# Sixteen modulation columns in a feed-forward: single-column sums on TensorE against transposes and a sum on VectorE

## The chip, the cores and the metric

The kernel runs on one core of one Trainium2 chip. The metric is the device time of one execution in microseconds (us). A core has five engines that run their own instruction streams and wait for each other through semaphores: PE (TensorE, matrix products into the eight PSUM banks), DVE (VectorE), ACT (ScalarE), POOL (GpSimd) and SP (SyncE, which here only issues transfers).

## The reference, cut to what matters

Two two-layer blocks with a width of 1024 follow each other on 512 tokens. Each layer multiplies and shifts its input by vectors that come from a condition vector `c` through a large matrix. The feed-forward of each layer of the first block is followed by a norm whose output is modulated by the *next* layer's first two vectors:

```python
c_act = jax.nn.silu(c)
for i in range(DEPTH):
    mods = jnp.split(c_act @ w_ada[i] + b_ada[i], 6, axis=-1)
    sh1, sc1, g1, sh2, sc2, g2 = [m[:, None, :] for m in mods]
    u = x * (1.0 + sc1) + sh1
    ...
    x = layer_norm(DEEPNORM_ALPHA * x + (1.0 + g1) * y, ln_g[i, 0], ln_b[i, 0])
    u = x * (1.0 + sc2) + sh2
    y = squared_relu_mlp(u, ff_w1[i], ff_w2[i])
    x = layer_norm(DEEPNORM_ALPHA * x + (1.0 + g2) * y, ln_g[i, 1], ln_b[i, 1])
```

The second block (`ada_w_2`, `ada_b_2`) uses shift, scale and gate in the same way after an RMS norm.

## The kernel before, in words

**Products.** Every float32 product is made of three TensorE passes (`PASSES`), with weights and activations split into a high and a low part. Weights come in halves of 512 rows by 512 columns: SP loads `raw`, ACT makes the high part (`act_high`, L191), POOL the low part (L2462), PE uses both (`wsp`), and `w_used` frees the slot.

**Modulation.** The product of `c` and the modulation matrix is not made on TensorE alone. While a feed-forward runs, DVE accumulates row block after row block, times the elements of silu(c), into `modacc[l]` (128 partitions by 6144 columns, L711). What is left is the sum over the 128 partitions. For shift and scale it must come out as *columns* (element on the partition), 16 blocks of 128 for each feed-forward. `pe_modcols` (L718) makes each with one product of the block with a column of ones; the trace has two records (passes) for each of these float32 products. For gates it must come out as *rows* on all partitions: `pe_modrow` (L724), ones times the accumulator.

**End of a feed-forward.** `pe_ff(l)` ends with `down_pair`: the last two blocks of the hidden layer (operands `hT` and `xT`) are multiplied into the two column halves n = 0 and n = 1 of the output, four token tiles t each. For n = 0 the results lie in banks 4 to 7, for n = 1 in banks 0 to 3; a tile of n = 1 is 24 products (L493). `down_tile` weaves the 16 `pe_modcols` into the 24 products of tile 0 of n = 1, one ahead of each of the first 16. They write bank 4, so PE waits for `ada_used` (all of `modacc` is there) and for `acc_done` of tile 0 of n = 0 (DVE is done with bank 4). The last one raises `mod_done`.

**DVE beside it.** `dve_ff` handles the tiles in the order that PE makes them: `add_pair(n, t)` adds what was accumulated (L652), multiplies by the gate (L653), adds the residual (L654), raises `acc_done` and takes norm statistics (L767). Between the four tiles of n = 0 and the four of n = 1 stands `before_pair`: `next_columns` waits for `mod_done` and adds the bias to the 16 columns from bank 4 (L2616), then a few operations on 8 columns fold them with the norm's scale and bias (L775 to L778 in the first feed-forward, L2630 to L2632 in the second), and `mod_made` is raised. The last tile of n = 1 has its sum prepared (`settled`) and begins with L653. In the second feed-forward alone, each tile of n = 1 is followed by `affine1` on DVE (L2674 and L2676, 1024 columns each), with which ACT makes the RMS norm.

**After it.** PE waits for `mod_made`, then does `pe_modrow` for both gates, and in the second feed-forward, once DVE has done `acc_done` of the very last tile, 16 further `pe_modcols` (L550). Then `pe_transposes_by_tile` turns the normed tokens (L339), in the second feed-forward with a wait for `mod_made` before k = 3, which DVE raises after another `next_columns` and the four operations of `next_rows` (L2625). After the transposes the products of the next stage start (L233).

Of the kernel before, what the change touches and what calls it, by code (L numbers as in the profile page):

```python
# [12 lines left out]
P = 128  # L13
# [34 lines left out]
def build(nc, T, out):  # L48
# [8 lines left out]
    with ctx:  # L57
# [43 lines left out]
        def col(name, k=0, n=1):  # L101
            return cols[:, ROWS[name] + k:ROWS[name] + k + n]
# [305 lines left out]
        def sp_ff(sp, l, ada, rows):  # L408
# [44 lines left out]
            for n in range(2):  # L453
                for q in range(2):
                    k = (FB - 2 + q) * HK
                    sp_half(sp, b + 4 * FB - 4 + 2 * n + q, q, W2[l][:, k:k + HK, n * COLS:n * COLS + COLS])
                    if n == 0:
                        ada_tiles(FB - 1, range(4 + 2 * q, 6 + 2 * q))

        def pe_ff(pe, l):  # L460
            s = FS[f"ff{l}"]
            b = base[f"ff{l}"]
            ts = TS[f"hid_ff{l}"]

            def up(m, peel=False):

                j = b if peel else b + 4 * m - 2
                if peel:
                    first_half(pe, j, "T", ts["bank_free"], 0, ts)
                for h in range(1 if peel else 0, 2):  # L470
                    for t in range(4):
                        if h == 0:
                            pe.wait_ge(s["sq_done"], 4 * m - 4 + t + 1)
                        for k in range(HK):
                            if t == 0:
                                low_ready(pe, j + h, k)
                            if peel and t == 0:
                                pe.wait_ge(ts["xT_ready"], ts["k0"] + HK * h + k + 1)
                            mm = pe_tile(pe, bank[t][:, :], h, k, HK * h + k, t, "T", h == 0 and k == 0,
                                         h == 1 and k == HK - 1)  # L480
                        if h == 1 and t < 3:
                            mm.then_inc(s["ff1_tile"], 1)
                    mm.then_inc(w_used, 1)

            def down_tile(h, j, slot, t, bk, start=True, stop=True, columns=()):
                for k in range(HK):
                    if t == 0:
                        low_ready(pe, j, k)
                    for q, (a, c) in enumerate(PASSES):
                        n = 3 * k + q  # L490
                        if n < len(columns):
                            pe_modcols(pe, modacc[l], columns[n:n + 1], ST, mod_done if columns[n] == 15 else None)
                        mm = pe.matmul(bank[bk][:, :], h[:, a, k, t * P:t * P + P], wsp[:, slot, c, k, :],  # L493
                                       start=(start and k == 0 and q == 0), stop=(stop and k == HK - 1 and q == 2))
                return mm

            def down(i, peel=False):

                j = b + 4 * i + 4
                pe.wait_ge(s["hT_ready"], 4 * i + 4)  # L500
                for n in range(2):
                    for t in range(ST):
                        if not (peel and n == 0):
                            pe.wait_ge(s["acc_done"], 8 * i + 4 * n - 4 + t + 1)
                        mm = down_tile(hT[l], j + n, n, t, ST + t)
                        mm.then_inc(s["ff2_tile"] if t < 3 else w_used, 1)

            def down_pair():

                i, j = FB - 2, b + 4 * FB - 4  # L510
                for q, h in enumerate((hT[l], xT)):
                    pe.wait_ge(s["hT_ready"], 4 * (i + q) + 4)
                    for t in range(ST):
                        if q == 0:
                            pe.wait_ge(s["acc_done"], 8 * i - 4 + t + 1)
                        mm = down_tile(h, j + q, q, t, ST + t, q == 0, q == 1)
                        if t == ST - 1:
                            mm.then_inc(w_used, 1)
                        elif q == 1:
                            mm.then_inc(s["ff2_tile"], 1)  # L520
                pe.wait_ge(s["sq_done"], 4 * FB)
                for t in range(ST):
                    for q, h in enumerate((hT[l], xT)):
                        columns = ()
                        if t == 0:
                            if q == 0:
                                pe.wait_ge(s["ada_used"], KT * FB)
                                pe.wait_ge(s["acc_done"], 8 * i + 1)
                            columns = (range(12), range(12, 16))[q]
                        mm = down_tile(h, j + 2 + q, q, t, t, q == 0, q == 1, columns)  # L530
                        if t == ST - 1:
                            mm.then_inc(w_used, 1)
                        elif q == 1:
                            mm.then_inc(s["ff2_tile"], 1)

            up(0, peel=True)
            up(1)
            down(0, peel=True)
            with pe.Fori(1, FB - 2) as i:
                up(i + 1)  # L540
                down(i)
            up(FB - 1)
            down_pair()
            pe.wait_ge(mod_made, (5, 8)[l])
            for r, off in enumerate(mod_rows[l]):
                pe.wait_ge(s["acc_done"], 8 * (FB - 2) + 2 * r + 2)
                pe_modrow(pe, modacc[l], off, ST + 2 * r, mod_done)
            pe.wait_ge(s["acc_done"], 8 * (FB - 2) + 2 * ST)
            if l:
                pe_modcols(pe, modacc[l], range(24, 40), HK - 1, mod_done, at=SEQ - P)  # L550
# [2008 lines left out]
        def _(dve):  # L2559
# [52 lines left out]
            def next_columns(at, bk, bias, done, off=0):  # L2612

                c = slice(at, at + 16)
                dve.wait_ge(mod_done, done)
                dchain(dve, dve.tensor_tensor(modcol[:, c], bank[bk][:, off + at:off + at + 16], bias, ALU.add))  # L2616

            def next_rows(l, one, done):

                dve.wait_ge(brow_ld, 32 * l + 32)  # L2620
                for r, gate in enumerate((gate1, gate2)):
                    dve.wait_ge(mod_done, done + r)
                    for n in range(2):
                        c = slice(n * COLS, n * COLS + COLS)
                        dchain(dve, dve.scalar_tensor_tensor(gate[:, c], bank[4 + 2 * r + n][:, :], one, brow[l][:, r, c], ALU.add, ALU.add))  # L2625
                dve.sem_inc(mod_made, 1)
# [14 lines left out]
            ready = TS["in_att_in"]["tok_ready"]  # L2641

            def before_pair0():
                next_columns(0, ST, col("b_ada", 48, 16), 5)
                dve_fold(dve, 0, 1, 0, 8)
                dve.sem_inc(mod_made, 1)
            dve_ff(dve, 0, 0, 1, gate2, 32, before_pair0, None)
# [16 lines left out]
            dve_transposed(dve, "hid_ff1")  # L2664

            def before_pair1():
                next_columns(0, ST, col("ada_b_2", 0, 16), 9)
                rms_fold(0)
                dve.sem_inc(mod_made, 1)
                dve.wait_ge(ln_ld, 128)  # L2670
# [75 lines left out]
```

## Time and profile before

| | us |
|---|---|
| median of 3 runs | 1802.36 |
| lowest and highest of them | 1799.96 and 1802.83 |
| the profiled execution's own time | 1807.33 |
| its span, first to last instruction | 1805.6 |
| mean granted TensorE clock of the span | 0.991 of full |

In the timeline each row is a group of like instructions: its start, the time to the end of the group, engine, line and operation, the tile written and those read, and how many. In square brackets stands how long the engine had been idle, and what ended that. PE is the product itself, PEld the loading of its stationary operand, which overlaps with the product before. Products are pipelined, so consecutive products start closer together than one takes. An engine's name with a q is its instruction queue.

### The profile page before, as it was taken

Reading aid. Unit: us, or ns where it says so; the run is one execution under the profiler, and the core shown is the slowest. Engines: PE = TensorE matmul, PEld = TensorE weight load, DVE = VectorE, ACT = ScalarE, POOL = GpSimd, SP = SyncE. Lnnn points to the kernel's source line nnn. Section 1 sums busy time; section 2 is a strip of 40 time slices with the busy share of each in tenths; the row PEclk is TensorE's granted clock in tenths of the full one; section 3 lists DMA queues with packets and bytes.
Section 4 is the critical chain, followed back from the end, with each engine's and each line's share of the span. In section 5 each row is a group of like instructions: output and inputs, shape, how many; then the busy total and the mean of one; then the engine's idle time right before and its main releaser. Section 6 shows DMA issues by size and latency. Waiting matters only on the chain.

```text
span 1805.6 us, 24893 instructions
## 1 busy us (share of the span) xinstructions
PE 1759.9 (97%) x9203; PEld 1445.3 (80%) x9203; DVE 1092.5 (61%) x1644; ACT 759.4 (42%) x1193; POOL 766.9 (42%) x577
## 2 busy tenths in 40 slices
PE   6999999999999999999999999999999999999999
PEld 5776677888888887888788888888888887887887
DVE  6876556656665772754475566568388845347742
ACT  3443336222222253664432222235444456665551
POOL 4523234555555354222355555552432334441222
PEclk9999999999999999999999999999999999999999
DMA  9643424655555323222275555542221132232211
GB/s 329 237 151 107 162 94 140 221 163 165 174 167 196 124 94 114 85 82 67 74 261 177 172 175 167 175 153 71 94 70 54 47 95 93 94 94 82 71 59 70
DMA packets 132219, 235.79 MB, mean 131 GB/s; under 512 B 8560, under 2 KB 48368, under 8 KB 132128
## 3 DMA queue, kind: packets, MB, share of 16 engines
q1 hardware_dynamic: 129088, 227.21, 38.3%
q10 hardware_dynamic: 3040, 7.34, 1.2%
q8 instruction: 61, 1.00, 0.2%
q14 instruction: 30, 0.25, 0.0%
HBM read 232.39 MB, written 2.13 MB: 130 GB/s over the span
## 4 chain that ended last, share of the span: by engine, by line
issue 44%; POOL 29%; PE 23%; DVE 3%; ACT 1%; POOLq 0%; DVEq 0%; ACTq 0%
POOL wsp L2462 29%; PE bank L233 12%; PE bank L1462 2%; PE bank L1428 2%; PE bank L1430 1%; PE bank L2009 1%; PE bank L1550 1%; PE bank L1538 1%; PE bank L1504 1%; PE bank L1763 0%; DVE hst L2248 0%; ACT fP L1584 0%; PE bank L1780 0%; DVE hE L2205 0%; DVE hX L2216 0%
## 5 line engine op out<-in xcount | busy, mean ns | idle before, releaser
L2462 POOL TENSOR_TENSOR wsp<-raw,wsp 128x512 fp32r<-128x512 f32 x528 | 758.9, 1468 | 1018.9 <-ACT wsp L191 1018.9
L233 PE MATMUL bank<-xT,wsp 128*128 128x512 f32 x2592 | 603.2, 392 | 4.3 <-ACT xT L379 2.7
L233 PEld LDWEIGHTS bank<-xT,wsp 128*128 128x128 f32 x2592 | 488.2, 189 | 109.7 <-DVE xT L385 3.2
L191 ACT ACTIVATE wsp<-raw 128x2048 fp32r<-128x2048 f32 x132 | 252.7, 1915 | 484.2 <-PE bank L493 240.8
L493 PE MATMUL bank<-wsp,hT 128*128 128x512 f32 x1344 | 313.4, 391 | 0.0
L233 PE MATMUL bank<-wsp,xT 128*128 128x512 f32 x1248 | 300.9, 396 | 2.2 <-POOL wsp L2462 2.0
L493 PEld LDWEIGHTS bank<-wsp,hT 128*128 128x128 f32 x1344 | 252.4, 188 | 51.4
L233 PEld LDWEIGHTS bank<-wsp,xT 128*128 128x128 f32 x1248 | 231.5, 189 | 55.7 <-issue 4.5
L634 DVE TENSOR_TENSOR x<-bank,x 128x512 f32<-128x512 f32 x80 | 55.3, 691 | 117.1 <-PE bank L493 116.7
L618 DVE TENSOR_TENSOR hT<-h,hT 128x512 fp32r<-128x512 f32 x56 | 90.5, 1674 | 23.4 <-ACT hT L568 23.4
L1428 PE MATMUL bank<-xT,wsp 128*128 128x512 f32 x384 | 99.3, 403 | 2.0 <-DVE gT L1930 2.0
L711 DVE SCALAR_TENSOR_TENSOR modacc<-ada_ring,csil,modacc 128x768 f32<-128x768 f32 (+1 forms) x80 | 91.5, 1143 | 3.4
L385 DVE TENSOR_TENSOR xT<-u,xT 128x512 fp32r<-128x512 f32 x64 | 65.0, 1036 | 44.5 <-ACT xT L379 44.3
L563 ACT ACTIVATE h<-bank 128x512 f32<-128x512 f32 x64 | 38.4, 599 | 114.3 <-PE bank L233 114.3
L1428 PEld LDWEIGHTS bank<-xT,wsp 128*128 128x128 f32 x384 | 68.9, 188 | 19.0 <-issue 2.9
L607 DVE TENSOR_TENSOR h<-bank,h 128x512 f32<-128x512 f32 x64 | 42.8, 686 | 65.6 <-ACT h L563 65.6
L711 DVE SCALAR_TENSOR_TENSOR tok<-ring,csil,tok 128x512 f32<-128x512 f32 x56 | 53.8, 960 | 10.5 <-DMA ring<-in_w_ada 5.0
L1430 PE MATMUL bank<-wsp,xT 128*128 128x256 f32 x384 | 50.0, 286 | 0.0
L1430 PEld LDWEIGHTS bank<-wsp,xT 128*128 128x128 f32 x384 | 46.9, 191 | 1.4 <-issue 1.4
L493 PE MATMUL bank<-wsp,xT 128*128 128x512 f32 x192 | 46.8, 393 | 0.0
L1584 ACT ACTIVATE fP<-fP,f_max 128x256 f32<-128x256 f32 (+3 forms) x64 | 35.3, 553 | 23.8 <-DVE f_max L1634 23.8
L1634 DVE CUSTOM_DVE_ANT_0 aP<-bank,abt 128x256 f32<-128x256 f32 (+3 forms) x64 | 27.5, 487 | 26.9 <-PE bank L1504 26.6
(319 smaller groups left out, 2044.1 us busy)
## 6 DMA issues: line engine op xcount, KB each, us to landing
raw<-in_ff_w SPq DMA_DIRECT2D x64, 1024.0 KB, 5.4
ada_ring<-in_w_ada SPq DMA_DIRECT2D x48, 384.0 KB, 3.8
ada_ring<-in_ada_w SPq DMA_DIRECT2D x48, 384.0 KB, 3.8
ring<-in_w_ada SPq DMA_DIRECT2D x64, 256.0 KB, 3.2
raw<-in_odd_w_in SPq DMA_DIRECT2D x16, 1024.0 KB, 5.5
raw<-in_gla_w_in SPq DMA_DIRECT2D x12, 1024.0 KB, 6.9
raw<-in_att_w_in SPq DMA_DIRECT2D x12, 1024.0 KB, 5.1
raw<-in_even_w_in SPq DMA_DIRECT2D x12, 1024.0 KB, 5.1
```

The source lines that it names most:

```text
L191: act.activation(wsp[:, slot, 0], raw[:, slot], ACT.Copy).then_inc(hi_made, 1)
L233: mm = pe.matmul(out_ap, l, r, start=(start and n == 0), stop=(stop and n == 2))
L385: dve.tensor_tensor(xT[:, 1, k], u32[:, k % 2], xT[:, 0, k].bitcast(F32), ALU.subtract)\
L493: mm = pe.matmul(bank[bk][:, :], h[:, a, k, t * P:t * P + P], wsp[:, slot, c, k, :], start=(start and k == 0 and q == 0), stop=(stop and k ...
L563: act.activation(h32[l][:, t], bank[t][:, :], ACT.Relu).then_inc(s["relu_done"], 1)
L607: dve.tensor_tensor(h32[l][:, t], bank[t][:, :], h32[l][:, t], ALU.mult).then_inc(s["sq_done"], 1)
L618: dve.tensor_tensor(h[:, 1, t], h32[l][:, t], h[:, 0, t].bitcast(F32), ALU.subtract)\
L634: ins = dve.tensor_tensor(y, bank[4 + t][:, :], y, ALU.add)
L711: ins = dve.scalar_tensor_tensor(acc, w, c, acc, ALU.mult, ALU.add)
L1428: mm = pe.matmul(bank[D_BANK][:, :], w[:, i * P:i * P + P], xT[:, a, k, :], start=start, stop=stop)
L1430: mm = pe.matmul(bank[D_BANK][:, 0:COLS // 2], xT[:, a, k, i * P:i * P + P], w, start=start, stop=stop)
L2462: ins = pool.tensor_tensor(wsp[:, slot, 1, k], raw[:, slot, k], wsp[:, slot, 0, k].bitcast(F32), ALU.subtract)
```

## The change

In both feed-forwards of the first block the 16 single-column products are no longer woven into tile 0 of n = 1. Instead PE transposes the 16 blocks of `modacc`, four to a bank, into banks 4 to 7, between tile 0 and tile 1 of n = 1. Each bank waits for the `acc_done` of its own tile of n = 0. DVE sums each transposed block along its free axis, with one `tensor_reduce` for a bank, and then adds the bias. The other 32 uses of `pe_modcols` (16 in the attention stage, 16 at the end of the second feed-forward) stay.

```diff
+        def pe_blocks_turned(pe, acc, bk, n):
+
+            for b in range(4 * n, 4 * n + 4):
+                at = b % 4 * P
+                mm = pe.transpose(bank[bk][:, at:at + P], acc[:, b * P:b * P + P], ident[:, :])
+            return mm
+
...
-            def down_tile(h, j, slot, t, bk, start=True, stop=True, columns=()):
+            def down_tile(h, j, slot, t, bk, start=True, stop=True):
                 for k in range(HK):
                     if t == 0:
                         low_ready(pe, j, k)
                     for q, (a, c) in enumerate(PASSES):
-                        n = 3 * k + q
-                        if n < len(columns):
-                            pe_modcols(pe, modacc[l], columns[n:n + 1], ST, mod_done if columns[n] == 15 else None)
...
                 pe.wait_ge(s["sq_done"], 4 * FB)
                 for t in range(ST):
+                    if t == 1:
+                        pe.wait_ge(s["ada_used"], KT * FB)
+                        for n in range(ST):
+                            pe.wait_ge(s["acc_done"], 8 * i + n + 1)
+                            mm = pe_blocks_turned(pe, modacc[l], ST + n, n)
+                        mm.then_inc(mod_done, 1)
                     for q, h in enumerate((hT[l], xT)):
-                        columns = ()
-                        if t == 0:
-                            if q == 0:
-                                pe.wait_ge(s["ada_used"], KT * FB)
-                                pe.wait_ge(s["acc_done"], 8 * i + 1)
-                            columns = (range(12), range(12, 16))[q]
-                        mm = down_tile(h, j + 2 + q, q, t, t, q == 0, q == 1, columns)
+                        mm = down_tile(h, j + 2 + q, q, t, t, q == 0, q == 1)
...
+            def first_columns(bias, done):
+
+                dve.wait_ge(mod_done, done)
+                for n in range(ST):
+                    blocks = bank[ST + n].rearrange("p (b n) -> p b n", n=P)
+                    ins = dve.tensor_reduce(modcol[:, 4 * n:4 * n + 4], blocks, AX, ALU.add)
+                dchain(dve, ins)
+                dchain(dve, dve.tensor_tensor(modcol[:, 0:16], modcol[:, 0:16], bias, ALU.add))
+
...
             def before_pair0():
-                next_columns(0, ST, col("b_ada", 48, 16), 5)
+                first_columns(col("b_ada", 48, 16), 5)
...
             def before_pair1():
-                next_columns(0, ST, col("ada_b_2", 0, 16), 9)
+                first_columns(col("ada_b_2", 0, 16), 9)
```

## Rows read from the trace of the kernel before

**Rows 1.** The page, busy time and share of the span by engine.

```profile
PE 1759.9 (97%) x9203; PEld 1445.3 (80%) x9203; DVE 1092.5 (61%) x1644; ACT 759.4 (42%) x1193; POOL 766.9 (42%) x577
```

**Rows 2.** Timeline of the first feed-forward's end, PE and DVE.

```profile
611.53 0.28 PE L718 MATMUL bank<-ones,modacc 128*128 128x1 f32 x2
...
617.34 0.69 DVE L654 SCALAR_TENSOR_TENSOR tok<-tok,bank 128x512 f32<-128x512 f32 x1
...
618.33 0.28 PE L718 MATMUL bank<-ones,modacc 128*128 128x1 f32 x2
...
618.79 0.17 DVE L2616 TENSOR_TENSOR modcol<-bank,cols 128x16 f32<-128x16 f32 x1
...
620.63 2.89 PE L493 MATMUL bank<-wsp,hT 128*128 128x512 f32 x12
620.84 0.70 DVE L652 TENSOR_TENSOR bank<-bank,x 128x512 f32<-128x512 f32 x1 [1.06 <-PE bank L493]
...
626.08 2.88 PE L493 MATMUL bank<-wsp,hT 128*128 128x512 f32 x12
626.28 0.70 DVE L652 TENSOR_TENSOR bank<-bank,x 128x512 f32<-128x512 f32 x1 [2.13 <-PE bank L493]
...
637.16 0.70 DVE L653 TENSOR_TENSOR bank<-bank,gate 128x512 f32<-128x512 f32 x1 [2.13 <-PE bank L493]
...
640.39 1.91 PE L339 MATMUL bank<-ident,tok 128*128 128x128 f32 x16
```

**Rows 3.** Timeline of the second feed-forward's end, PE and DVE.

```profile
1222.29 0.28 PE L718 MATMUL bank<-ones,modacc 128*128 128x1 f32 x2
...
1229.55 0.17 DVE L2616 TENSOR_TENSOR modcol<-bank,cols 128x16 f32<-128x16 f32 x1
...
1231.66 0.70 DVE L652 TENSOR_TENSOR bank<-bank,x 128x512 f32<-128x512 f32 x1 [1.33 <-PE bank L493]
...
1237.41 0.69 DVE L652 TENSOR_TENSOR bank<-bank,x 128x512 f32<-128x512 f32 x1
...
1247.72 3.59 PE L724 MATMUL bank<-modacc,ones 128*128 128x512 f32 x8
...
1248.88 0.69 DVE L653 TENSOR_TENSOR bank<-bank,gate 128x512 f32<-128x512 f32 x1
...
1249.61 0.69 DVE L654 SCALAR_TENSOR_TENSOR tok<-tok,bank 128x512 f32<-128x512 f32 x1
...
1251.15 3.63 PE L718 MATMUL bank<-ones,modacc 128*128 128x1 f32 x32
...
1252.68 1.28 DVE L2676 SCALAR_TENSOR_TENSOR x<-tok,rstd,lnrow 128x1024 f32<-128x1024 f32 x1
...
1254.82 0.17 DVE L2616 TENSOR_TENSOR modcol<-bank,cols 128x16 f32<-128x16 f32 x1 [0.85 <-PE bank L718]
...
1255.03 2.87 DVE L2625 SCALAR_TENSOR_TENSOR gate<-bank,brow 128x512 f32<-128x512 f32 x4
...
1258.00 4.53 PE L339 MATMUL bank<-ident,tok 128*128 128x128 f32 x20 [0.68 <-DVEq L2626]
...
1262.19 28.09 PE L233 MATMUL bank<-xT,wsp 128*128 128x512 f32 x122
```

**Rows 4.** Groups by line and form, and one timeline row: prices on DVE.

```profile
L767 DVE BATCH_NORM_STATS2 stats<-tok 128x6 f32<-128x512 f32 x32 | 22.2, 695 | 1.1
...
L2274 DVE TENSOR_TENSOR_SCAN u<-ones,hu 128x512 f32<-128x512 f32 x4 | 4.9, 1215 | 0.0
...
1273.84 0.48 DVE L2181 MEMSET u<- 128x512 f32 x1 [0.17 <-DVE omlb L2175]
```

**Rows 5.** Windows: stretch, length, busy time by engine, granted clock, DMA.

```profile
640.00:645.00 5.00, 4.66 (x37) 4.06 (x36) 3.47 (x6) 4.93 (x9) 3.96 (x4) 1.00 0.00 0
...
1255.50:1256.00 0.50, 0.36 (x3) 0.08 (x1) 0.47 (x2) 0.47 (x2) 0.50 (x1) 0.65 0.00 0
...
1262.00:1262.50 0.50, 0.50 (x4) 0.50 (x3) 0.00 (x0) 0.50 (x2) 0.00 (x0) 0.52 1.05 410
```

## The prediction

> **What bounds the kernel now.** I read the page first: PE is busy for 97% of the span [rows 1], so the first question about any edit is what it does to PE's stream. Then I read the timeline at the end of each feed-forward, because the edit acts at two places only, and asked there which wait ends last.
>
> In the first feed-forward PE goes from product to product without a gap, and DVE waits for it: 1.06 us before tile 0 of n = 1, 2.13 us before tile 1 and 2.13 us before the last one [rows 2]. PE sets the pace. A tile of n = 1 takes PE 626.08 - 620.63 = 5.45 us; DVE needs 3.3 us for it (626.28 - 2.13 - 620.84).
>
> In the second feed-forward it is the other way round. DVE has `affine1` behind each tile, so that its tiles start 1237.41 - 1231.66 = 5.75 us apart, more than PE's 5.45, and DVE idles only ahead of the first, 1.33 us [rows 3]. From there to the end of the feed-forward DVE has no rest. After it the path is: DVE's last tile, PE's 16 late column sums (1251.15, which could not start before `acc_done` of L654, ended 1250.30), DVE's L2616 (it waited 0.85 us for them), L2625 until 1257.90, and only then PE's 20 transposes and the next stage at 1262.19 [rows 3]. So a microsecond saved on PE counts in the first feed-forward, while in the second one added on DVE before 1231.66 counts.
>
> **What is removed.** 16 column sums, 32 passes, from each feed-forward. Tile 0 of n = 1 takes 620.63 - 611.53 = 9.10 us instead of 5.45 [rows 2], so they cost 3.65 us, 0.114 us a pass. The 32 passes that stand alone took 3.63 us [rows 3], the same price, so the weaving hides nothing and costs nothing. DVE's bias add remains.
>
> **What is added on PE.** 16 transposes of 128 x 128. The nearest row is the 16 float32 transposes of `tok`, 1.91 us from first start to last end [rows 2]. A single one took about 0.28 us, but they overlap: (1.91 - 0.28) / 15 = 0.11 us from one to the next, so 16 displace 1.8 us. I take 1.8 us and as bounds 1.7 and 2.2 (if a switch between products and transposes costs some tenths). Saved on PE: 3.65 - 1.8 = 1.85 us in each feed-forward.
>
> A rule speaks against this: the Trainium skill, page "TensorE: Matmul & The Clock Gate", Part 4 (PE-mode transpose), gives about 275 ns for a transpose in a kernel. Taken as the displaced time that would be an estimated 4.4 us for 16, dearer than the 3.65 us removed, and the first feed-forward would lose 0.75 us. The trace has that length for one record but not from start to start, so I keep the row.
>
> **The new waits on PE.** The fourth bank waits for `acc_done` of tile 3 of n = 0, whose L654 ended at 618.03 [rows 2]. Without the woven passes tile 0 ends at 611.53 + 5.45 = 616.98; twelve transposes later, at 618.3, the thirteenth is due. The bank is free 0.3 us earlier: no stall. The second feed-forward has the same distances, with tile 0 starting at 1222.29 [rows 3]. If DVE were later than that, tiles 1 to 3 of n = 1 would queue behind the wait, and DVE's tile 1 behind them.
>
> **What is added on DVE.** Four reductions over 512 float32 from PSUM. The trace before has no such operation. Near rows: operations with 512 columns took 0.69 to 0.70 us, from PSUM too (L652) [rows 2, 4]. Below stands a write of 512 without reading, 0.48; above stands a scan with its serial dependence, 1.215 [rows 4]. I take 0.69, because a sum along the axis reads a column per step as the statistics (0.695) do: 2.8 us for four, bounds 1.9 and 4.9. The wait moves as well: the last transpose ends at 616.98 + 1.8 + 0.2 = 619.0. Then 2.8, bias add and fold (619.78 - 618.79 = 1.0 for L2616 to L778, which end 1.06 us ahead of 620.84) give 622.85, where DVE can take tile 0 of n = 1. It began it at 620.84, so it is 2.0 us late.
>
> **First feed-forward: -1.85 us.** PE's tile 1 is ready for DVE at 626.28 - 1.85 = 624.43, DVE comes at 626.15 (622.85 + 3.3); tile 2 is ready at about 629.9 and DVE is free at 629.5: it has caught up. The last tile begins 1.85 us earlier. Even with reductions of 1.215 us (2.1 us more) DVE would be free at 634.9, ahead of the last tile at 637.16 - 1.85 = 635.3. The cover is thick here. Everything behind it up to the second feed-forward is triggered by PE and its followers (the weight transfers too, through `lo_made`), so it shifts as a whole.
>
> **Second feed-forward, with the clock as it was: +1.3 us.** Times are on the old axis. The last transpose ends at 1222.29 + 5.45 + 1.8 + 0.2 = 1229.75, the reductions at 1232.55, bias and three fold operations 0.8 later, and tile 0 starts at 1233.4 against 1231.66: +1.75 us. With 5.75 us a tile and no rest, the last tile is late by the same: L654 ends at 1252.05 instead of 1250.30, L2676 at 1255.7 instead of 1253.96. PE, 1.85 us early, ends its row sums (L724) at 1249.45 and then *waits* for that `acc_done`: a gap of 2.6 us that was not there. The 32 passes then run from about 1252.5 to 1256.1, L2616 follows at 1256.1 instead of 1254.82, and with it L2625 and PE's 20 transposes: +1.3 us. Of DVE's 1.75 us the old idle 0.85 hid the rest. PE's 1.85 us is lost in the new gap.
>
> **The clock in that gap: +2.0 us.** The granted clock fell to 0.5 (1.2 GHz) at about 1255.8 and came back at 1262.2 to 1262.5 [rows 5]. Before it fell PE had finished its wide products at 1251.3 and done only single columns and transposes. In it the 20 transposes took 4.53 us, twice the 0.11 us each. Now the wide products end 1.85 us earlier. If the clock falls as long after them as it did (4.5 us), that is at 1253.95, when about 2.1 us of the late column sums are still to do; at half clock those take twice as long, +2.1. If it falls as late as before it costs nothing; if it falls before the sums, 3.6. I take 2.0.
>
> **Sum.** -1.85 + 1.3 + 2.0 = +1.5 us. Against the profiled execution's own time that is 1807.3 to 1808.8; this execution lies 5.0 us above the median of the runs, so on the median it is 1802.4 + 1.5 = 1803.9. From no change a measurement of this kernel tells about 0.2%, 3.6 us.
>
> **Rivals.**
> 1. *Both feed-forwards gain.* DVE's delay in the second is hidden after all and PE's 1.85 us counts twice: -3.7 us, 1798.7. For it: DVE idles 1.33 us before tile 0 of n = 1 [rows 3]. Against it: the delay of 1.75 is reckoned after that idle time, and no rest follows. Chance 0.05.
> 2. *The clock stays out of it*, or is back earlier for the 20 transposes (2.3 instead of 4.5 us): -0.55 to -2.7 us, 1799.7 to 1801.8. For it: the moment of the fall can differ from one execution to the next. Chance 0.15.
> 3. *The reductions are slow, and this ends slower.* DVE's price decides: each 0.1 us above 0.69 adds 0.4 us in the second feed-forward. From 1.2 us on a reduction the total passes +3.6 us; at the scan's 1.215 it is 1.5 + 2.1 = +3.6 us, 1806.0, and still above if the first tile is late as well. Against it: three kinds of operation with 512 columns took 0.69. Chance 0.08.
> 4. *The clock falls ahead of the late sums and stays low through the transposes:* 3.6 instead of 2.0, and up to 1.5 us more until it is back: +3.1 to +4.6 us, 1805.5 to 1807.0. Chance 0.12.
> 5. *The transposes themselves make the clock fall within tile 1 of n = 1.* If one tile of n = 1 fell to 1.2 GHz for its 5.45 us, half of that would be lost work, 2.7 us: the first feed-forward's gain is gone, +4.2 us in all, 1806.6. The transposes between 640 and 645, in which PE did little else, ran at a granted 1.00 [rows 5], and here only half as many stand between wide products. Chance 0.03.
>
> The page named above says in the same part that transposes do not count as TensorE being busy for the clock gate. By that rule the fifth rival would be likelier; the trace shows a stretch of transposes at full clock, and a fall where waits stood beside them.
>
> **How the numbers follow.** The forecast, the sums caught in part by the fall, has 0.57 and holds -0.55 to +3.1 us. With rivals 2 and 4 and the halves of 3 and 5 that stay below 3.6 us the middle is thick: within 0.2% 0.83. Faster by over 0.2% is rival 1 and a little of 2: 0.05. Slower is the upper part of 3, 4 and 5: 0.12. The range goes from 1799.8 (rival 2's lower part) to 1806.6 (rival 4's upper part); it leaves out rival 1 and the slow tail, and what other executions' clock elsewhere adds.
>
> **What the changed profile would show.** L718 with 64 records instead of 128; two bursts of 16 transposes at about 1.8 us; tile 0 of n = 1 at 5.45 us; four reductions at 0.69 us each; in the first feed-forward no idle PE and DVE waiting again from tile 2; in the second DVE's four tiles with no idle time, PE idle for 2.6 us ahead of the late L718, and these at more than 0.114 us a pass if the clock fell in them. Wrong are: the sign, if DVE's L652 of the second feed-forward starts at less than 1.3 us late; the size, if a reduction is not near 0.69 us or the fall is elsewhere; the first step, if PE stalls on the fourth bank.

## The result, and the profile after

The changed kernel is slower: 1811.72 us median of 6 runs (1809.1 to 1814.0) against 1802.46 us for the kernel before (6 runs, 1799.72 to 1804.05). The ratio is 1.0047, 95% interval 1.0035 to 1.006. The forecast was 1803.9 us, the range 1799.8 to 1806.6 us, and the likeliest outcome no change beyond 0.2%. The time is above all of it, and there is a change. The first line of the page shows nothing of this; PE is even busy for 2 us less than before [rows 1]:

```profile
PE 1757.9 (97%) x9171; PEld 1443.3 (80%) x9171; DVE 1096.2 (61%) x1652; ACT 759.7 (42%) x1193; POOL 768.0 (42%) x577
```

The profiled execution's span is 1808.7 us, 3.1 us above that of before. Both spans hold what the clock did to unchanged code, so I compare *stages*: a stage here is the stretch from DVE's first gate product of n = 0 (L653, in the changed kernel L657) to the first product of what follows (L233), once for each feed-forward. For before, four further rows of the timeline give both starts, the end of the first stage and, between them, POOL:

```profile
607.85 0.70 DVE L653 TENSOR_TENSOR bank<-bank,gate 128x512 f32<-128x512 f32 x1
...
613.78 4.99 POOL L2462 TENSOR_TENSOR wsp<-raw,wsp 128x512 fp32r<-128x512 f32 x4 [4.30 <-ACT wsp L191]
...
644.36 1.86 PE L233 MATMUL bank<-xT,wsp 128*128 128x512 f32 x7
...
1218.61 0.70 DVE L653 TENSOR_TENSOR bank<-bank,gate 128x512 f32<-128x512 f32 x1
```

The two stages take 644.36 - 607.85 = 36.51 us and, with the last row of [rows 3], 1262.19 - 1218.61 = 43.58 us. Now the timeline of the changed kernel at the end of the first feed-forward:

```profile
602.12 0.70 DVE L657 TENSOR_TENSOR bank<-bank,gate 128x512 f32<-128x512 f32 x1
...
605.80 2.88 PE L497 MATMUL bank<-wsp,hT 128*128 128x512 f32 x12
...
608.06 5.00 POOL L2466 TENSOR_TENSOR wsp<-raw,wsp 128x512 fp32r<-128x512 f32 x4 [4.29 <-ACT wsp L191]
...
609.39 0.96 PE L497 MATMUL bank<-wsp,xT 128*128 128x512 f32 x3 [0.70 <-POOL wsp L2466]
...
610.63 0.96 PE L497 MATMUL bank<-wsp,xT 128*128 128x512 f32 x3 [0.28 <-POOL wsp L2466]
...
611.87 0.96 PE L497 MATMUL bank<-wsp,xT 128*128 128x512 f32 x3 [0.28 <-POOL wsp L2466]
...
613.11 0.97 PE L497 MATMUL bank<-wsp,xT 128*128 128x512 f32 x3 [0.27 <-POOL wsp L2466]
...
613.92 1.91 PE L464 MATMUL bank<-ident,modacc 128*128 128x128 f32 x16
615.58 3.01 PE L497 MATMUL bank<-wsp,hT 128*128 128x512 f32 x12
615.93 2.48 DVE L2627 TENSOR_REDUCE modcol<-bank 128x4 f32<-128x512 f32 x4 [2.91 <-PE bank L464]
...
632.23 0.70 DVE L657 TENSOR_TENSOR bank<-bank,gate 128x512 f32<-128x512 f32 x1 [2.13 <-PE bank L497]
...
639.44 0.94 PE L233 MATMUL bank<-xT,wsp 128*128 128x512 f32 x3
```

Read the four rows of PE with "POOL wsp" at their end. The second half of tile 0 needs the low parts of a weight half that POOL makes one by one, in pieces k = 0 to 3 of three products each, and PE now waits ahead of each piece. Tile 0 takes 613.92 - 605.80 = 8.12 us, not 5.45. POOL works at the same times as before, counted from DVE's first gate product: it begins 5.94 us after it (before 613.78 - 607.85 = 5.93) and ends 10.94 us after it (before 10.92). Tile 1 begins at 13.46 us instead of 620.63 - 607.85 = 12.78. The stage takes 639.44 - 602.12 = 37.32 us: 0.81 us more, where 1.85 less was forecast.

The second feed-forward:

```profile
1215.44 0.70 DVE L657 TENSOR_TENSOR bank<-bank,gate 128x512 f32<-128x512 f32 x1
...
1226.41 0.97 PE L497 MATMUL bank<-wsp,xT 128*128 128x512 f32 x3 [0.28 <-POOL wsp L2466]
...
1227.22 1.91 PE L464 MATMUL bank<-ident,modacc 128*128 128x128 f32 x16
...
1229.23 2.48 DVE L2627 TENSOR_REDUCE modcol<-bank 128x4 f32<-128x512 f32 x4 [2.90 <-PE bank L464]
...
1232.77 0.70 DVE L656 TENSOR_TENSOR bank<-bank,x 128x512 f32<-128x512 f32 x1 [0.23 <-DVE bcol L2645]
...
1249.98 0.69 DVE L657 TENSOR_TENSOR bank<-bank,gate 128x512 f32<-128x512 f32 x1
...
1251.45 5.87 PE L722 MATMUL bank<-ones,modacc 128*128 128x1 f32 x32 [2.53 <-DVE tok L658]
...
1257.36 0.17 DVE L2620 TENSOR_TENSOR modcol<-bank,cols 128x16 f32<-128x16 f32 x1 [2.29 <-PE bank L722]
...
1260.55 3.56 PE L339 MATMUL bank<-ident,tok 128*128 128x128 f32 x20 [0.56 <-DVEq L2639]
...
1263.86 2.32 PE L233 MATMUL bank<-xT,wsp 128*128 128x512 f32 x9
```

DVE takes its first tile of n = 1 at 1232.77 - 1215.44 = 17.33 us instead of 13.05, 4.28 us late, and has no idle time from there to the end of its last tile. That tile is late by the same, PE waits 2.53 us for it, and the late column sums start 36.01 us after the first gate product instead of 32.54 and take 5.87 us instead of 3.63. The 20 transposes behind them are faster by 0.9 us. The stage takes 48.42 us, 4.84 more. The windows show the granted clock in it (the last number but two of a line, 1.00 for 2.4 GHz and 0.50 for 1.2 GHz):

```profile
1252.00:1252.50 0.50, 0.50 (x7) 0.50 (x6) 0.43 (x4) 0.50 (x1) 0.00 (x0) 1.00 0.00 0
1252.50:1253.00 0.50, 0.50 (x6) 0.50 (x5) 0.50 (x2) 0.49 (x2) 0.00 (x0) 0.71 0.00 0
...
1262.50:1263.00 0.50, 0.50 (x5) 0.50 (x4) 0.50 (x1) 0.50 (x2) 0.00 (x0) 0.55 0.95 365
...
1389.00:1389.50 0.50, 0.50 (x6) 0.50 (x5) 0.50 (x2) 0.00 (x0) 0.00 (x0) 0.74 0.13 33
```

The clock falls to 1.2 GHz at about 1252.7, early in the late sums, and is back at about 1262.9. The last line is a further fall, near 1389, in code that the change does not touch. The first fall has not moved toward the start of the stage: it lies 37.3 us after the first gate product, in before at 37.0. It is the late sums that have moved into it.

### The profile page after: what moved, and what is told of

It is laid out like the page before. It is cut to its first block, busy times and chain, and to the rows that moved or that the text cites. A ratio compares the mean times of both kernels' runs of the same rounds, so it can differ in the third digit from the quotient of the medians.

```text
span 1808.7 us, 24837 instructions
## 1 busy us (share of the span) xinstructions
PE 1757.9 (97%) x9171; PEld 1443.3 (80%) x9171; DVE 1096.2 (61%) x1652; ACT 759.7 (42%) x1193; POOL 768.0 (42%) x577
## 3 DMA queue, kind: packets, MB, share of 16 engines
HBM read 232.39 MB, written 2.13 MB: 130 GB/s over the span
## 4 chain that ended last, share of the span: by engine, by line
issue 43%; POOL 29%; PE 22%; DVE 3%; ACT 1%; POOLq 0%; DVEq 0%; ACTq 0%
POOL wsp L2466 29%; PE bank L233 11%; PE bank L1466 2%; PE bank L1432 2%; PE bank L1434 1%; PE bank L2013 1%; PE bank L1554 1%; PE bank L1542 1%; PE bank L1508 1%; PE bank L1767 0%; DVE hst L2252 0%; ACT fP L1588 0%; PE bank L1784 0%; DVE hE L2209 0%; DVE hX L2220 0%
## 5 line engine op out<-in xcount | busy, mean ns | idle before, releaser
L233 PE MATMUL bank<-xT,wsp 128*128 128x512 f32 x2592 | 602.8, 392 | 4.3 <-ACT xT L379 2.8
L233 PEld LDWEIGHTS bank<-xT,wsp 128*128 128x128 f32 x2592 | 488.1, 189 | 108.9 <-DVE xT L385 2.9
L497 PE MATMUL bank<-wsp,hT 128*128 128x512 f32 x1344 | 308.5, 389 | 0.0
L233 PE MATMUL bank<-wsp,xT 128*128 128x512 f32 x1248 | 300.0, 395 | 2.3 <-POOL wsp L2466 2.0
L233 PEld LDWEIGHTS bank<-wsp,xT 128*128 128x128 f32 x1248 | 230.7, 188 | 55.5 <-issue 4.5
L1434 PEld LDWEIGHTS bank<-wsp,xT 128*128 128x128 f32 x384 | 46.9, 191 | 1.4 <-issue 1.4
L497 PEld LDWEIGHTS bank<-wsp,xT 128*128 128x128 f32 x192 | 35.4, 188 | 13.4 <-POOL wsp L2466 6.5
L1588 ACT ACTIVATE fP<-fP,f_max 128x256 f32<-128x256 f32 (+3 forms) x64 | 35.2, 553 | 23.8 <-DVE f_max L1638 23.8
```

The lines of the kernel that those rows point to most:

```text
L233: mm = pe.matmul(out_ap, l, r, start=(start and n == 0), stop=(stop and n == 2))
L1434: mm = pe.matmul(bank[D_BANK][:, 0:COLS // 2], xT[:, a, k, i * P:i * P + P], w, start=start, stop=stop)
```

## The experiments

Stages in us from the timelines, as above; "first tile" is DVE's start of n = 1 in the second feed-forward after its first gate product; "between" and "behind" are the stretches between the stages and from the second one to the end. Ratios with 95% intervals; behind them stand runs of before on the same chip, with medians of 1802.5 to 1803.7 us.

| kernel | stage 1 | between | first tile | stage 2 | behind | ratio to before |
|---|---|---|---|---|---|---|
| before | 36.51 | 574.25 | 13.05 | 43.58 | 543.41 | |
| after | 37.32 | 576.00 | 17.33 | 48.42 | 544.84 | 1.0047 (1.0035 to 1.006) |
| same_again | 36.51 | 573.84 | 13.05 | 43.48 | 543.26 | 1.0007 (0.9995 to 1.0019) |
| one_column | 35.52 | 575.83 | 12.06 | 42.59 | 543.89 | 1.0011 (0.9996 to 1.0026) |
| only_first | 37.31 | 573.86 | 13.05 | 43.53 | 543.25 | 1.0014 (1.0004 to 1.0023) |
| only_second | 36.51 | 573.76 | 17.33 | 48.41 | 544.92 | 1.0032 (1.0018 to 1.0045) |
| in_tile | 35.55 | 575.48 | 14.80 | 44.26 | 544.73 | 0.9999 (0.9988 to 1.0009) |
| in_tile_first | 35.57 | 574.43 | 13.05 | 43.57 | 543.37 | 1.0001 (0.999 to 1.0011) |
| no_reduce | 37.29 | 573.71 | 14.81 | 44.26 | 544.78 | 1.0015 (1.0004 to 1.0027) |
| after_again | 37.32 | 575.65 | 17.32 | 48.40 | 544.81 | 1.0048 (1.0035 to 1.0061) |
| filled_gap | 37.28 | 575.96 | 17.32 | 48.41 | 544.83 | 1.0033 (1.0014 to 1.0052) |
| extra_reduce | 36.51 | 571.96 | 14.47 | 43.91 | 544.82 | 1.0014 (1.0001 to 1.0027) |
| one_reduce | 36.51 | 573.83 | 13.05 | 43.54 | 544.69 | 1.0009 (0.9994 to 1.0024) |
| eight_reduce | 36.51 | 571.97 | 16.98 | 48.04 | 543.13 | 1.0035 (1.002 to 1.0051) |

The stages come out alike within 0.1 us wherever their code is alike, which no whole time does. The conclusions rest on them.

**same_again**, the kernel before without an edit.

> The kernel before, unchanged, as a control. Expected: a ratio of 1.000 within 0.1%. Question: do the stretches at 1.2 GHz in its trace fall at the same places as in the first trace of before (150 to 164, 229 to 236, 283 to 287, 836 to 839, 894 to 898, 1256 to 1262)? If they are tied to the place in the program, the same six are seen. If they are a matter of the single execution, some are missing, and the span differs from 1805.6 us by what they cost.

The stages are the same, the falls of the clock are not: those near 157 and 283 us are missing, one near 101 is new, and its span is 1801.7 us against 1805.6. The falls in the unchanged first 600 us are a matter of the execution. The four traces of before, below, have spans of 1799.1 to 1805.6 us, so that a single span tells nothing of a difference below some 6 us.

**one_column**: is the removed work worth anything?

```diff
-                            columns = (range(12), range(12, 16))[q]
+                            columns = ((), range(15, 16))[q]
```

> The kernel before with 15 of the 16 woven column sums left out in both feed-forwards (only column 15 is made, ahead of the first product of tile 0's second half; the other columns keep whatever the bank held). Theory POOL: the weave stands in a hole in which PE would wait for POOL's low halves anyway, so leaving out 30 passes (3.4 us) shortens tile 0 of n = 1 by only about 1 us (9.1 to about 8.1 us), PE is seen waiting for POOL in its second half, and the kernel is about 2 us faster in all. Rival, the prediction's step: tile 0 shrinks by 3.4 us to about 5.7 us, DVE starts the tiles of n = 1 earlier by up to 1.3 us, and the kernel is 5 us faster.

PE in the first feed-forward:

```profile
605.95 2.88 PE L493 MATMUL bank<-wsp,hT 128*128 128x512 f32 x12
...
609.53 0.38 PE L718 MATMUL bank<-ones,modacc 128*128 128x1 f32 x2 [0.70 <-POOL wsp L2462]
...
613.25 0.96 PE L493 MATMUL bank<-wsp,xT 128*128 128x512 f32 x3 [0.27 <-POOL wsp L2462]
614.05 2.89 PE L493 MATMUL bank<-wsp,hT 128*128 128x512 f32 x12
```

Tile 0 takes 614.05 - 605.95 = 8.1 us with 3.4 us less to do. Both stages are 0.99 us shorter, no more. So the removed weave was worth 1.0 us of PE's time in each feed-forward, not 3.65. The 2 us that this should save in all do not appear in the timing, and noise does not cover them: they would be a ratio of 0.9989, below the interval. The trace has 575.83 us between the stages, where a fall of the clock near 830 lasts 6.8 us instead of the 3.4 us in before; whether that goes with this kernel or with the one execution is open.

**only_first** and **only_second**: the change in one feed-forward alone, by `l == 0` or `l == 1` around the new lines, the woven sums in the other.

> The change in the first feed-forward alone. Theory POOL: tile 0 of n = 1 takes 8.3 us because its second half waits for POOL, the transposes come behind that, and the start of the attention stage's products is 0.75 us later, measured from the start of tile 0; the kernel is 0.5 to 2.5 us slower, the rest by where the clock falls. Rival, the prediction's step: 1.85 us faster.

> The change in the second feed-forward alone. Theory: nearly all of the loss is here. DVE starts the tiles of n = 1 about 4.5 us late (2.9 us wait of PE for POOL, 1.8 us for transposes and 2.5 us for reductions, less 2.7 us that the weave used beyond), stays late by the same because it has no rest, and with the late column sums partly at 1.2 GHz the next stage starts 5 us later: kernel 5 to 7 us slower. Rival: the loss lies in stretches at 1.2 GHz elsewhere, then this kernel is under 3 us slower.

The stages are those of the changed kernel in the edited feed-forward and those of before in the other. The first costs 0.8 us, the second 4.8 to 4.9, and the ratios stand in the same order.

**in_tile**: the transposes inside tile 0.

```diff
             for k in range(HK):
+                if turn:
+                    turn(k)
                 if t == 0:
                     low_ready(pe, j, k)
...
+                def turn(n):
+                    pe.wait_ge(s["acc_done"], 8 * i + n + 1)
+                    mm = pe_blocks_turned(pe, modacc[l], ST + n, n)
+                    if n == ST - 1:
+                        mm.then_inc(mod_done, 1)
...
-                        mm = down_tile(h, j + 2 + q, q, t, t, q == 0, q == 1)
+                        mm = down_tile(h, j + 2 + q, q, t, t, q == 0, q == 1, turn if t == 0 and q == 1 else None)
```

> The changed kernel with the transposes moved into tile 0 of n = 1: the four of bank n stand ahead of the products with k = n of the second half, where PE waits for POOL's low halves. Theory POOL: they are hidden in those waits. Tile 0 takes 8.1 us, as with one woven column; the first feed-forward's stage (from DVE's first L653 of n = 0 to the next stage's first product) takes 35.5 us instead of 37.3 with the change and 36.5 before. In the second, DVE starts the tiles of n = 1 2.9 us earlier than with the change and the stage takes 44.5 to 45.5 instead of 48.4 (before 43.5). Kernel within 0.1% of before. Rival (transposes cost their 1.8 us wherever they stand): 37.3 stays in the first.

```profile
610.55 2.89 PE L499 MATMUL bank<-wsp,hT 128*128 128x512 f32 x12
...
614.94 0.60 PE L464 MATMUL bank<-ident,modacc 128*128 128x128 f32 x4
...
615.38 0.96 PE L499 MATMUL bank<-wsp,xT 128*128 128x512 f32 x3
...
618.67 2.91 PE L499 MATMUL bank<-wsp,hT 128*128 128x512 f32 x12
```

Tile 0 with all 16 transposes in it takes 8.12 us, as long as the changed kernel's tile 0 has without them. There they cost nothing. Stage 1 is 1.77 us shorter than the changed kernel's. What the change loses on PE is the place of the transposes: behind POOL's last piece instead of between the pieces.

**in_tile_first**: that place in the first feed-forward, the woven sums in the second.

> The first feed-forward as in the kernel with transposes in tile 0, the second as before the change (woven column sums). Theory POOL: stages of 35.5 and 43.5 us, 1.0 us less than before in the sum, a ratio of 0.9995, which a timing can't tell from 1. Rival (the prediction's arithmetic, by which the whole 1.85 is gained): 34.7 in the first.

35.57 and 43.57 us: the shortest sum of all kernels that leave nothing out, 0.85 to 0.95 us less than in the traces of before. The timing can't tell it from before.

**no_reduce**: DVE's addition by itself.

```diff
-                for n in range(ST):
-                    blocks = bank[ST + n].rearrange("p (b n) -> p b n", n=P)
-                    ins = dve.tensor_reduce(modcol[:, 4 * n:4 * n + 4], blocks, AX, ALU.add)
-                dchain(dve, ins)
-                dchain(dve, dve.tensor_tensor(modcol[:, 0:16], modcol[:, 0:16], bias, ALU.add))
+                dchain(dve, dve.tensor_tensor(modcol[:, 0:16], bank[ST][:, 0:16], bias, ALU.add))
```

> The changed kernel with the four reductions left out in both feed-forwards: the bias is added to the first 16 columns of bank 4, whatever they hold. PE's work is unchanged. Theory: the reductions cost 2.5 us of DVE only in the second feed-forward; there DVE starts the tiles of n = 1 2.5 us earlier (14.8 instead of 17.3 us after its first L653 of n = 0) and the stage takes 45 to 46 us instead of 48.4; the first stays at 37.3. Rival (PE's late tile 0 alone is the cause): both stages stay as with the change.

Stage 1 does not move: there the reductions are free. In the second, the first tile comes 2.5 us earlier. Stage 2 falls to 44.26, even below the expected 45 to 46. So does that of in_tile, which has the reductions but not PE's delay. Each cause alone makes the first tile 1.75 us late and costs 0.7 us; together they make it 4.28 us late and cost 4.84. The first part of a delay goes into idle time that was there, 1.33 us before the first tile and 0.85 us before the late bias add [rows 3]; the second part finds none left. The clock adds the rest. With either cause alone the late sums start 0.9 us later than before and take 4.36 us (no_reduce) or 4.03 us (in_tile), but the clock is back earlier in the transposes behind them, which get back more than the sums lose. With both, the sums start 3.47 us later and take 5.87 us, and the transposes get back only 0.9 us of the 2.24.

**eight_reduce**, **extra_reduce** and **one_reduce**: the kernel before with eight, four or one added reductions on DVE in the second feed-forward, and nothing else. With four:

```diff
+                dve.wait_ge(mod_done, 9)
+                for n in range(ST):
+                    blocks = bank[ST + n].rearrange("p (b n) -> p b n", n=P)
+                    ins = dve.tensor_reduce(ctmp[:, 4 * n:4 * n + 4], blocks, AX, ALU.add)
+                dchain(dve, ins)
                 next_columns(0, ST, col("ada_b_2", 0, 16), 9)
```

> The kernel before with four reductions over 512 columns (into a scratch tile, not used) added on DVE between the last column sum and the bias add of the second feed-forward alone. Theory DVE: 2.5 us more, of which the idle 1.3 us take the half; DVE starts the tiles of n = 1 at 14.3 us instead of 13.05, the last is 1.2 us later, and the stage takes 43.9 to 44.8 us instead of 43.5, since part of it lies in the 0.85 us in which DVE waited for the late sums. Open, with no forecast: whether a fall of the clock near 1385 to 1391 us shows up, which all five traces with the second feed-forward changed have and none of the five without.

> As the kernel with four added reductions, but with one (0.6 us). Theory DVE: it fits in the 1.3 us in which DVE waited before its first tile of n = 1, so that nothing moves: 13.05 and 43.5 us as before. And if the 1.5 us that all seven traces with a longer second stage show behind it (544.8 instead of 543.3 us from there to the end) come from the shift and not from the edit, they are absent: 543.3.

> As the kernel with four added reductions, but with eight (5 us). Theory DVE: DVE starts the tiles of n = 1 at 16.9 to 17.0 us and never has rest again, the last at 34.1 to 34.2, and PE has a gap of about 3 us before the late column sums, at an unchanged tile 0 and without any transpose. Stage 47 to 48.5 us, almost that of the changed kernel, which would show that the delay of DVE alone makes the loss there. Ratio 1.002 to 1.004.

One is hidden, four cost 0.3 to 0.4 us, eight cost 4.46 to 4.56. With eight, PE's work and tile 0 are those of before, and there is no transpose of `modacc`. PE's rows behind its row sums:

```profile
1247.50 6.99 PE L718 MATMUL bank<-ones,modacc 128*128 128x1 f32 x32 [2.98 <-DVE tok L654]
1254.35 2.80 PE L339 MATMUL bank<-ident,tok 128*128 128x128 f32 x12
```

The first tile is 3.93 us late here, against 4.28 in the changed kernel. So a delay of DVE alone gives the gap on PE, the slow late sums and the long stage.

**filled_gap**: is it the gap that makes the clock fall?

```diff
+                if l and r:
+                    for n in range(2):
+                        pe.matmul(bank[ST + 2 * r + n][:, :], ones[:, :], modacc[l][:, off + n * COLS:off + n * COLS + COLS],
+                                  start=True, stop=True)
                 pe_modrow(pe, modacc[l], off, ST + 2 * r, mod_done)
```

> The changed kernel with the second gate's row sums of the second feed-forward made twice: four more passes of 512 columns (1.7 us) into the same banks with the same values. They fill 1.7 of the 2.5 us in which PE waits for DVE's last tile. PE has more work, nothing waits for less. Theory clock: the gap makes the clock fall earlier, inside the 16 late column sums (5.9 us with the change, 3.6 before). Filled, the clock falls later, the sums take 3.6 to 4.5 us and the stage of the second feed-forward 46.5 to 47.5 us instead of 48.4. Rival: the sums are slow for another reason, or the fall stands where it stood; then the stage stays at 48.4.

```profile
1252.38 1.88 PE L732 MATMUL bank<-modacc,ones 128*128 128x512 f32 x4
1255.06 5.87 PE L726 MATMUL bank<-ones,modacc 128*128 128x1 f32 x32 [0.80 <-DVE tok L662]
```

The gap is down to 0.80 us, wide products run until 1254.26, and the sums still take 5.87 us, the stage still 48.41. My theory of the clock is refuted: the idle time in the gap does not set when the clock falls. The windows of the other traces say the same. All times but the last column are in us after the first gate product of the second feed-forward:

| trace | last wide product ends | late sums start | clock falls | clock is back | late sums take |
|---|---|---|---|---|---|
| before | 32.7 | 32.5 | 37.0 | 43.9 | 3.63 |
| same_again | 32.7 | 32.5 | 36.6 | 43.4 | 3.63 |
| no_reduce | 33.5 | 33.5 | 36.4 | 43.2 | 4.36 |
| after | 33.5 | 36.0 | 37.3 | 47.5 | 5.87 |
| after_look2 | 33.5 | 36.0 | 36.6 | 46.9 | 6.47 |
| filled_gap | 35.2 | 36.0 | 37.3 | 47.5 | 5.87 |
| eight_reduce | 32.7 | 35.7 | 35.7 | 45.9 | 6.99 |

In no_reduce there is no gap at all, and the clock still falls within the sums. The fall stays at 35.7 to 37.3 us in all eighteen traces, while what stands there changes; what sets it no run shows. The time at 1.2 GHz is 10.2 us instead of 6.8 in the kernels whose sums start at 35.7 us or later. In the changed kernel it didn't matter where the fall was: after and after_look2 have late sums of 5.87 and 6.47 us, and the transposes behind take back the difference, so that both stages are 48.4 us.

**after_again**, **after_look1**, **after_look2**, **before_look1** and **before_look2**: the stages account for 5.65 of the 8.5 us that the ratio stands for; where is the rest? These are the two kernels again, without an edit.

> The changed kernel, unchanged, for a second trace and a narrower ratio. The two stages together are 5.65 us longer than before. If the rest of the measured 0.47% (8.5 us) is a matter of where the clock falls in an execution, the ratio comes out between 1.003 and 1.004 and the stages at 37.3 and 48.4 again; if it belongs to the change, it is 1.0045 or more, and the trace shows again a fall near 1389 us and a long one near 830 us.

> The kernel before, unchanged, for a further trace. If the stretch between the two feed-forward stages (573.8 to 574.3 us so far, without change in its code) and the rest behind the second (543.3 to 543.4 us) belong to the kernel, they come out as before; if they are a matter of the execution, one of the two traces of before shows 575.5 or more, or 544.7.

> As the trace of before beside it: 573.8 to 574.3 and 543.3 us if these stretches belong to the kernel, 575.5 or 544.7 in some execution if not.

> The changed kernel, unchanged, for a further trace. The stages come out at 37.3 and 48.4 us. If the longer stretches of the two traces so far (575.7 to 576.0 us between the stages, 544.8 us behind) belong to the kernel, they come again, with a fall of the clock near 830 of 6.8 us and one near 1390; if not, one of the two traces of after shows 573.8 or 543.3.

> As the trace of after beside it: 575.7 to 576.0 and 544.8 us if these stretches belong to the kernel, 573.8 or 543.3 in some execution if not.

| trace | to stage 1 | stage 1 | between | stage 2 | behind | span |
|---|---|---|---|---|---|---|
| before | 607.85 | 36.51 | 574.25 | 43.58 | 543.41 | 1805.6 |
| same_again | 604.61 | 36.51 | 573.84 | 43.48 | 543.26 | 1801.7 |
| before_look1 | 605.14 | 36.50 | 573.91 | 43.56 | 543.19 | 1802.3 |
| before_look2 | 601.82 | 36.51 | 573.94 | 43.57 | 543.26 | 1799.1 |
| after | 602.12 | 37.32 | 576.00 | 48.42 | 544.84 | 1808.7 |
| after_again | 604.22 | 37.32 | 575.65 | 48.40 | 544.81 | 1810.4 |
| after_look1 | 607.55 | 37.27 | 573.86 | 48.40 | 544.82 | 1811.9 |
| after_look2 | 607.05 | 37.32 | 573.84 | 48.41 | 544.78 | 1811.4 |

Behind the second stage all four traces of the changed kernel have 544.8 us and a fall near 1390, and all four of before have 543.2 to 543.4 and none there. So these 1.5 us come with the changed kernel, in unchanged code. Five of its relatives have the fall near 1390 too (only_second, in_tile, no_reduce, filled_gap and extra_reduce, 544.7 to 544.9 us), and the other five have not. The 2 us between the stages are a fall near 830 that lasts 6.8 us instead of 3.4 in two of the four traces of the changed kernel and in none of before; four traces don't decide whether they belong to the change. Without them the sum is 0.81 + 4.84 + 1.5 = 7.15 us, within the interval of the ratio, 0.35% to 0.6% or 6.3 to 10.8 us.

## Why the prediction was wrong, step by step

- **The step that failed** is "The 32 passes that stand alone took 3.63 us [rows 3], the same price, so the weaving hides nothing and costs nothing", and with it "tile 0 of n = 1 at 5.45 us". The equal price shows only that PE was busy all through the weave, not how long tile 0 lasts without it. I compared tile 0 with its neighbours without asking what it has and they have not: new weights. Only tile 0 waits in `low_ready`. In before there was no idle time to see, because the woven passes filled it. POOL's row ends at 618.77 (613.78 + 4.99), while tile 0 without the weave would have reached the last of the four pieces at about 616.3 (611.53 and 21 of 24 products in 5.45 us); that row was in the timeline, and the prediction has no row of POOL. Measured: the weave cost 1.0 us, not 3.65.
- *First feed-forward, -1.85 us.* It is +0.8: 1.0 saved, 1.8 added behind the hole. The price of the transposes was right (16 in 1.91 us). That DVE catches up was right too: it waits 2.13 us before the last tile again, and no_reduce leaves the stage unchanged.
- *The new waits on PE.* No stall on `acc_done`: right, but not for the margin of 0.3 us that was reckoned. PE came 2.65 us later than thought, so that nothing was close: in the first feed-forward the transposes start at 613.92, and the L658 for which the last bank waits had ended at 612.30.
- *DVE's price.* Four reductions in 2.48 us against 2.8 forecast: right, a little high.
- *Second feed-forward, +1.3 us.* The mechanism, DVE's delay with no rest behind it, was right, the size was not: DVE is 4.28 us late, not 1.75, for PE's transposes ended 2.65 us later than reckoned (reductions start 13.79 us after the first gate product, forecast 1229.75 - 1218.61 = 11.14). The claim that idle time hides part of 1.75 us is borne out by in_tile, with 0.7 us. The forecast also lets PE start the sums at 1252.5, 0.45 us after DVE's L654 at 1252.05; in the changed kernel it takes 0.05 (1251.45 after 1251.40). The gap of 2.53 us against the 2.6 forecast is luck: PE and DVE both came there about 2.6 us later than reckoned.
- *The clock, +2.0 us.* The late sums took 2.24 us more, near the forecast, but by luck. The reason given was that the fall comes earlier, with the wide products; it came no earlier, the sums came later, and filled_gap takes away most of the gap and changes nothing. With the delay that was forecast, 1.75 us, the sums took only 0.4 us (in_tile) and 0.7 us (no_reduce) more. And the 20 transposes behind them took 3.56 instead of 4.53 us [rows 3], since the clock came back in the midst of them, so that the clock cost 1.4 us in all (from their start to the first product behind them 3.31 instead of 4.19 us, 2.24 - 0.88 = 1.36).
- *The rivals.* None was the case as a whole; of the second, the earlier end of the slow clock in the 20 transposes was. That the transposes make the clock fall within tile 1 did not happen: tile 1 took 5.6 us in the first feed-forward (615.58 to 621.15), 0.1 us more than in before, at a granted clock of 1.00. That both gain is refuted by the stages. The chance of 0.83 for no change rested on bounds around known terms, and the missing one, 2.65 us of PE in each feed-forward, was in none.
- *Unforeseen:* 1.5 us behind the second stage. That it comes with the changed kernel is shown by four traces against four; why, is not. It isn't the delay of DVE as such: eight_reduce has the delay and 543.13 us, one_reduce has none and 544.69, with a fall near 1492 instead.

## What to carry to other kernels

A busy engine may be busy with filler, that is with work that stands where the engine would otherwise wait. Before you say what removing work saves, list the other things that the instructions behind it wait for, and when each is ready; here the row of a helper engine, POOL, for the next weights was the answer, and the missing idle time on PE said nothing. Put work that has its operands early into such holes rather than behind them. And in a stage that an engine runs without rest, idle time ahead of it is a budget: two additions that cost 0.7 us each by themselves cost 4.8 us together.

## What the runs showed of the hardware

- 16 float32 transposes of 128 x 128 displaced 1.8 us at 2.4 GHz, 0.11 us each, though a record is 0.27 us long. The Trainium skill gives about 275 ns for a bf16 one in a kernel ("TensorE: Matmul & The Clock Gate", Part 4); that agrees with the length of the float32 record here, not with what one costs in a burst.
- A `tensor_reduce` over 512 float32 in PSUM, into 4 columns, took 0.68 us a record and 2.48 us for four in a row.
- No kernel here differs from another before the first stage, and yet the time to it ranges from 601.8 us (before_look2) to 610.1 us (extra_reduce), with other falls of the clock. In places behind, a fall comes in every trace of one kernel and in none of another: near 1390 in four of four against none of four.
- In the second feed-forward the granted clock fell 4.3 us (before), 3.8 us (after), 2.1 us (filled_gap) and 5.4 us (one_column) behind the last wide product. No fixed distance holds, so such a fall can't be placed from one trace, as I tried. It needs no idle time either: in before and in no_reduce PE had none between the last wide product and the fall, only single columns and, in before, transposes.
